# Wide passes of neighbouring products back to back in a split-fp32 SwiGLU kernel: products four and five, and seven and the next first

## The chip, the cores and the metric

The kernel runs on one core of a Trainium2 chip. The metric is device time in microseconds (us) of one execution. Before the change it is 1697.6 us, the median of three runs (1697.36 to 1698.68).

## What is computed

One layer of a trunk: RMS norm, forgetting attention with four heads, residual, RMS norm, SwiGLU, residual, final RMS norm; 512 tokens, width 2048, inner width 5632, all float32. The change touches the first half of SwiGLU only:

```python
def _swiglu(h, w_gate_up, w_down):
    gu = h @ w_gate_up                      # (512, 2048) @ (2048, 11264)
    g, u = gu[..., :D_FF], gu[..., D_FF:]
    return (jax.nn.silu(g) * u) @ w_down
```

## The kernel before

**Split operands.** Every float32 operand is taken as a high part, rounded to the fast float32 format of TensorE (fp32r), and a low part, the remainder. A product is high weights by high tokens, high weights by low tokens, and low weights by high tokens. In gate and up a product has 256 tokens. Its *wide pass* (L3075) runs the high weights against 512 columns, the 256 tokens' high and low parts side by side, eight matmuls for eight blocks of 128 rows. Its *narrow pass* (L3081) runs the low weights against the 256 columns of the high parts, eight matmuls into the left half of the same PSUM bank.

**Units of seven products.** A unit computes 128 columns of gate and the same 128 of up, for all 512 tokens, with seven products in place of eight (a Strassen-Winograd scheme). The token side (`SEVEN`: A11, S1, S2, A12, S3, S4, A22) is made once; the trace names it hT, oT, oT, hT, s, nothing, hT. The weight side of each product (`PART_OF`) is a loaded block of 1024 x 128 or a sum of such blocks: B11 alone, B11+B12, that plus B22 (both sums by DVE, L2410), B21 alone, B12+B22 (by an accumulating DMA that POOL issues, L1151), B22 alone, and a last one again by POOL. There are 41 units in this form: one opens, 36 run in a loop of four units per turn (`Fori`), four are unrolled at the end. Three more are computed plainly before them (L3059 and L3064), with 512 columns in every matmul. The down product with 512 columns throughout (L3126) follows.

**Who does what, per product.**
- ACT rounds the weight block into the high ring buffer (`part_hi`, L1617). The ring has two places, so it waits until the wide pass of the product two before has read its place (`highs_read`) and until DVE has made that product's low part.
- DVE subtracts it from the block, which gives the low part (`part_lo`, L2399). It waits for the high part (`t_hi`) and until the product two before is complete (`product`, which the last narrow matmul raises), since the low ring also has two places.
- PE waits for `t_hi` before a wide pass and for `t_lo` before a narrow one, and at some products for a bank: `combined` (DVE's combinations of banks, L2428) or `q_copied` (ACT's copies, L1641 and L1649).
- Each engine's order is written out by hand in its own `unit`, and an engine runs it strictly in that order. DVE's is: low part 2 (`unit_lo(at, 1)`), second sum, gate's right half of the unit before, low part 3, the product of gate and up of the unit before with its small sums (L2475, L2452), low part 4, the combination for product three's bank, low parts 5 and 6, and so on; at the end low part 1 and the first sum of the next unit.
- SP issues the loads of later units when a low part is made (`load_after`): that of B22 for the next unit after low part 6, of B21 after low part 7.

Products are counted from one in this text and from zero in the code: product four is `e == 3`, and low part four is `unit_lo(at, 3)`.

The functions that the change touches, and what calls them:

Of the kernel before, what the change touches and what calls it, by code (L numbers as in the profile page):

```python
# [216 lines left out]
def fox_layer(nc, x, norm_mix, w_in, b_f, w_out, norm_ffn, w_gu, w_down, norm_out, out):  # L217
# [10 lines left out]
    G = 4  # L228
# [32 lines left out]
    with ExitStack() as ctx:  # L261
# [3 lines left out]
        def sem(name):  # L265
            return ctx.enter_context(nc.semaphore(name))
# [121 lines left out]
        SEVEN = ((A11, 0), (S1, 1), (S2, 0), (A12, 3), (S3, 0), (S4, 2), (A22, 0))  # L388
# [6 lines left out]
        def bank_of(at, which):  # L395

            return UNIT_BANKS[0 if at.r is None else (at.u + 1) % 2][which]
# [5 lines left out]
        def whole(bank):  # L403

            return ps[:, bank, :].rearrange("p (n t) -> p n t", n=2)
# [178 lines left out]
        def is_last(r):  # L584

            return isinstance(r, int) and r == GROUPS - 2
# [117 lines left out]
        combined = sem("combined")  # L704
# [1174 lines left out]
        def _(dve):  # L1879
# [521 lines left out]
            def named_lo(r, n, name, i):  # L2401
                part_lo(r, n, slot(place(r, name, i)[0]))

            def unit_lo(at, e):
                named_lo(at.r, at.first + e, PART_OF[e], at.u)
# [12 lines left out]
            def second_sum(at):  # L2418

                dve.wait_ge(t_lo, at.part(1))  # L2420
                wait_loaded(dve, at.r, "B22", at.u)
                sum_of(at, "B11", "B22")

            def bank(at, which):
                return ps[:, bank_of(at, which), :]

            def combine(out, in0, in1, op):
                nc.vector.tensor_tensor(out, in0, in1, op).then_inc(combined, 1)  # L2428
# [5 lines left out]
            def gate_right_before(at):  # L2434

                dve.wait_ge(x_taken, at.taken(0))
                add_right(ga[:, HALF:S], bank_before(at))

            def plain_out(f, into):

                dve.wait_ge(silu_done, f + 1)
                if f:
                    dve.wait_ge(product, 4 * f)
                else:
                    wait_used(dve, At(FIRST_FFN + 1))
                nc.vector.tensor_tensor(into, ps[:, GU[f % 2][1], :], into, ALU.mult).then_inc(a_done, 1)
# [38 lines left out]
            def unit(at):  # L2485

                end = is_last(at.r) and at.u == G - 1
                unit_lo(at, 1)
                second_sum(at)
                if at.r is not None:  # L2490
                    gate_right_before(at)
                    unit_lo(at, 2)
                    act_before(at)
                else:
                    plain_out(2, third)
                    dve.wait_ge(a_copied, 2)
                    first_of_pair(0, 0)
                    second_of_pair(0, 0)
                    unit_lo(at, 2)
                unit_lo(at, 3)  # L2500
                if at.r is None:
                    dve.wait_ge(a_copied, 3)
                    first_of_pair(1, 4)
                dve.wait_ge(product, at.product(2))
                dve.wait_ge(q_copied, at.copied(2))
                combine(bank(at, 2), qq[:], bank(at, 0), ALU.subtract)
                unit_lo(at, 4)
                unit_lo(at, 5)
                if end:
                    wait_loaded(dve, at.r, "B21", at.u)  # L2510
                    dve.wait_ge(t_lo, at.part(2))
                    sum_of(at, "B11", "B21")
                dve.wait_ge(x_taken, at.taken(1))
                add_right(ga[:, 0:HALF], bank_of(at, 3))
                dve.wait_ge(product, at.product(4))
                combine(qq[:], qq[:], bank(at, 0), ALU.subtract)
                unit_lo(at, 6)
                dve.wait_ge(a_done, at.acts())
                dve.wait_ge(combined, at.combined(3))
                combine(cc[:, HALF:S], qq[:, 0:HALF], qq[:, HALF:S], ALU.add)  # L2520
                if not end:
                    unit_lo(at.next(), 0)
                    first_sum(at.next())
                if end:
                    operand_low(Down(None, 0), 0)
                    operand_low(Down(None, 0), 1)
                    down_lo(Down(None, 0), 0)
                    gate_right_before(at.next())
                    down_sum(Down(None, 0), 0)
                dve.wait_ge(x_taken, at.taken(2))  # L2530
                add_right(cc[:, 0:HALF], bank_of(at, 2))
# [154 lines left out]
            for u in range(G):  # L2686
                unit(Unit(GROUPS - 2, u))

            first = Down(None, 0)
# [29 lines left out]
        def _(pe):  # L2719
# [187 lines left out]
            first = At(0)  # L2907
# [157 lines left out]
                                           start=False, stop=second == 1 and k == QK8 - 1)  # L3065
                ins.then_inc(product, 1)

            def half_product(at, e):

                tokens, which = SEVEN[e]  # L3070
                n = at.first + e
                both = whole(bank_of(at, which))
                pe.wait_ge(t_hi, at.part(e))
                for k in range(QK8):
                    ins = nc.tensor.matmul(both, ring(at.r, 0, n)[:, k * P:(k + 1) * P],  # L3075
                                           tokens[2][:, :, k * HALF:(k + 1) * HALF],
                                           start=e < 2 and k == 0, stop=False, skip_group_check=True)
                ins.then_inc(highs_read, 1)
                pe.wait_ge(t_lo, at.part(e))
                for k in range(QK8):  # L3080
                    ins = nc.tensor.matmul(both[:, 0, :], ring(at.r, 1, n)[:, k * P:(k + 1) * P],  # L3081
                                           tokens[0][:, k * HALF:(k + 1) * HALF],
                                           start=False, stop=k == QK8 - 1, skip_group_check=True)
                ins.then_inc(product, 1)

            def unit(at):

                first = at.r is None
                if first:
                    pe.wait_ge(silu_done, 2)  # L3090
                else:
                    pe.wait_ge(combined, at.combined(-5))
                half_product(at, 0)
                if first:
                    pe.wait_ge(a_done, 2)
                    pe.wait_ge(s_lo, 12)
                half_product(at, 1)
                pe.wait_ge(q_copied, at.copied(1))
                half_product(at, 2)
                half_product(at, 3)  # L3100
                pe.wait_ge(combined, at.combined(1))
                half_product(at, 4)
                if first:
                    pe.wait_ge(s_lo, 16)
                half_product(at, 5)
                pe.wait_ge(combined, at.combined(3))
                half_product(at, 6)

            def down_product(dn, e):

# [35 lines left out]
            at = At(FIRST_FFN)  # L3146
# [55 lines left out]
```

## Time and profile before

| | |
|---|---|
| median of three runs | 1697.6 us |
| the profiled execution, its own time | 1697.54 us |
| its span, first to last instruction | 1695.7 us |
| PE busy (matmuls) | 1682.6 us, 99% |
| PEld busy (weight loads) | 1449.5 us, 85% |
| DVE busy | 1337.2 us, 79% |
| ACT busy | 853.8 us, 50% |
| POOL busy | 210.6 us, 12% |
| granted TensorE clock, mean | 0.998 |
| gate and up in units of seven | 465.38 to 1267.04 us |

Busy times are shares of the span. Matmuls are pipelined: a matmul row shows how long one is under way, which is longer than the distance from one to the next, so the stream's pace is read from starts, or from the chain of waits, and not from the mean of one. A row that groups eight matmuls has the time from the first start to the last end. Brackets give idle time of that engine before the row and what ended it.

### The profile page before, as it was taken

How to read it: one execution, taken by the hardware profiler on the slowest of the kernel's cores; microseconds unless marked ns; L12 is line 12 of the kernel's file. 1: busy time of each engine (PE TensorE's matmuls, PEld its weight loads, DVE VectorE, ACT ScalarE, POOL GpSimd, SP SyncE). 2: the span in 40 equal slices, each digit the busy share in tenths (PEclk: the TensorE clock that was granted, in tenths of full speed). 3: DMA queues.
4: the chain of work that ended last, by engine and by line, in shares of the span. 5: the costliest groups of instructions: out<-in, count | busy, mean ns of one | idle time of the engine just before them, and what ended most of it. 6: DMA issues, size and time to landing. Idle time of an engine off the chain costs nothing.

```text
span 1695.7 us, 25155 instructions
## 1 busy us (share of the span) xinstructions
PE 1682.6 (99%) x8977; PEld 1449.5 (85%) x8977; DVE 1337.2 (79%) x1485; ACT 853.8 (50%) x1075; POOL 210.6 (12%) x327
## 2 busy tenths in 40 slices
PE   9999999999999999999999999999999999999998
PEld 7888888888888888888888888888888888888886
DVE  6888778968877777777777777777789978878886
ACT  6454555444445454445454445454455444444454
POOL 1010102001011111111111111111100001000043
PEclk9999999999999999999999999999999999999999
DMA  8746667942277777776777776777788886867854
GB/s 236 168 100 162 149 150 218 316 100 74 73 208 180 186 186 186 195 187 174 186 181 204 195 195 177 186 187 185 197 241 244 251 240 194 253 178 192 257 156 146
DMA packets 311630, 317.55 MB, mean 187 GB/s; under 512 B 10256, under 2 KB 259360, under 8 KB 305168
## 3 DMA queue, kind: packets, MB, share of 16 engines
q1 hardware_dynamic: 291968, 231.79, 44.2%
q0 software_dynamic: 19152, 83.37, 25.0%
q10 hardware_dynamic: 448, 1.55, 0.3%
q8 instruction: 40, 0.66, 0.2%
q14 instruction: 22, 0.18, 0.0%
HBM read 205.83 MB, written 30.41 MB: 139 GB/s over the span
## 4 chain that ended last, share of the span: by engine, by line
PE 74%; DVE 1%; issue 0%; ACT 0%; POOL 0%; POOLq 0%; ACTq 0%; DVEq 0%
PE ps L3075 31%; PE ps L3126 23%; PE ps L3081 16%; PE ps L3059 2%; PE ps L3064 1%; PE ps L3041 1%; DVE split L2540 0%; DVE down_slot L2553 0%; PE ps L3045 0%; ACT split L1726 0%; DVE tmp L1907 0%; PE ps L2737 0%; DVE xres L2569 0%; ACT xres L1607 0%; POOL var L1233 0%
## 5 line engine op out<-in xcount | busy, mean ns | idle before, releaser
L1617 ACT ACTIVATE split<-raw 128x1024 fp32r<-128x1024 f32 x295 | 312.1, 1058 | 342.5 <-DVE raw L2410 112.9
L2399 DVE TENSOR_TENSOR split<-raw,split 128x1024 fp32r<-128x1024 f32 x295 | 360.5, 1223 | 139.1 <-ACT split L1617 135.0
L3126 PE MATMUL ps<-split,operand_hi 128*128 128x512 f32 x1232 | 380.5, 389 | 0.2
L3126 PEld LDWEIGHTS ps<-split,operand_hi 128*128 128x128 f32 x1232 | 231.2, 188 | 49.8 <-ACT split L1726 0.9
L3075 PE MATMUL ps<-hT,split 128*128 128x512 f32 x984 | 246.4, 392 | 0.0
L3126 PE MATMUL ps<-split,operand_lo 128*128 128x512 f32 x616 | 239.7, 389 | 0.0
L1726 ACT ACTIVATE split<-down_slot 128x2048 fp32r<-128x2048 f32 (+1 forms) x82 | 145.6, 1781 | 173.9 <-PE ps L3126 84.8
L3075 PEld LDWEIGHTS ps<-hT,split 128*128 128x128 f32 x984 | 177.0, 189 | 31.7
L2540 DVE TENSOR_TENSOR split<-down_slot,split 128x2048 fp32r<-128x2048 f32 (+1 forms) x84 | 177.2, 2109 | 19.8 <-ACT split L1726 16.2
L3075 PE MATMUL ps<-oT,split 128*128 128x512 f32 x656 | 164.3, 392 | 0.0
L3081 PEld LDWEIGHTS ps<-hT,split 128*128 128x128 f32 x984 | 134.2, 190 | 9.6
L3081 PE MATMUL ps<-hT,split 128*128 128x256 f32 x984 | 137.2, 282 | 0.0
L3126 PEld LDWEIGHTS ps<-split,operand_lo 128*128 128x128 f32 x616 | 115.7, 188 | 24.0
L3075 PEld LDWEIGHTS ps<-oT,split 128*128 128x128 f32 x656 | 118.0, 189 | 21.1
L1150 POOL TENSOR_TENSOR turn_of<-half 128x1 f32<-128x1 f32 x81 | 31.7, 391 | 738.4 <-DVE raw L2410 302.6
L2569 DVE TENSOR_TENSOR xres<-xres,ps 128x1024 f32<-128x1024 f32 (+1 forms) x72 | 86.7, 1204 | 40.3 <-PE ps L3126 39.8
L2410 DVE TENSOR_TENSOR raw<-raw 128x1024 f32<-128x1024 f32 x83 | 101.7, 1226 | 7.8
L1381 ACT ACTIVATE split<-raw 128x1024 fp32r<-128x1024 f32 x63 | 66.7, 1060 | 61.4 <-DVE raw L2040 26.2
L3081 PEld LDWEIGHTS ps<-oT,split 128*128 128x128 f32 x656 | 89.5, 190 | 6.4
L3081 PE MATMUL ps<-oT,split 128*128 128x256 f32 x656 | 91.5, 282 | 0.0
L2034 DVE TENSOR_TENSOR split<-raw,split 128x1024 fp32r<-128x1024 f32 x63 | 76.8, 1221 | 17.9 <-ACT split L1381 17.9
L3075 PE MATMUL ps<-s,split 128*128 128x512 f32 x328 | 82.1, 392 | 0.0
(281 smaller groups left out, 2469.3 us busy)
## 6 DMA issues: line engine op xcount, KB each, us to landing
raw<-in_ffn_w_gate_up_dram SPq DMA_DIRECT2D x172, 512.0 KB, 5.0
raw<-raw POOLq DMA_DIRECT2D x99, 512.0 KB, 4.5
down_slot<-in_ffn_w_down_dram SPq DMA_DIRECT2D x32, 1024.0 KB, 7.1
a_sums<-pack SPq DMA_DIRECT2D x22, 1024.0 KB, 6.4
raw<-in_fox_w_in_dram SPq DMA_DIRECT2D x36, 512.0 KB, 4.7
down_slot<-down_slot POOLq DMA_DIRECT2D x16, 1024.0 KB, 8.1
operand_raw<-a_sums SPq DMA_DIRECT2D x28, 512.0 KB, 7.3
down_slot<-in_ffn_w_down_dram SPq DMA_DIRECT2D x16, 768.0 KB, 6.5
```

Of the source, the lines that this page charges most:

```text
L1381: nc.scalar.activation(head_ring(0, n), head_part(at, e), ACT.Copy).then_inc(u_hi, 1)
L1617: nc.scalar.activation(ring(r, 0, n), source, ACT.Copy).then_inc(t_hi, 1)
L1726: nc.scalar.activation(down_ring(dn, 0, e), down_part(dn, DOWN_OF[e]), ACT.Copy).then_inc(d_hi, 1)
L2034: nc.vector.tensor_tensor(head_ring(1, n), head_part(at, e), f32(head_ring(0, n)), ALU.subtract).then_inc(u_lo, 1)
L2399: nc.vector.tensor_tensor(ring(r, 1, n), source, f32(ring(r, 0, n)), ALU.subtract).then_inc(t_lo, 1)
L2410: nc.vector.tensor_tensor(x1, x1, x2, ALU.add).then_inc(t_sum, 1)
L2540: nc.vector.tensor_tensor(down_ring(dn, 1, e), down_part(dn, DOWN_OF[e]), f32(down_ring(dn, 0, e)), ALU.subtract).then_inc(d_lo, 1)
L2569: nc.vector.tensor_tensor(part, part, down_banks(dn, which)[:, tiles, :], ALU.add if sign > 0 else ALU.subtract).then_inc(y_added, 1)
L3059: ins = nc.tensor.matmul(out, ring(None, 0, n)[:, k * P:(k + 1) * P], h_ffn[part][:, :, QK8 * second + k, :], start=second == 0 and k == 0 ...
L3075: ins = nc.tensor.matmul(both, ring(at.r, 0, n)[:, k * P:(k + 1) * P], tokens[2][:, :, k * HALF:(k + 1) * HALF], start=e < 2 and k == 0, s ...
L3081: ins = nc.tensor.matmul(both[:, 0, :], ring(at.r, 1, n)[:, k * P:(k + 1) * P], tokens[0][:, k * HALF:(k + 1) * HALF], start=False, stop=k ...
L3126: ins = nc.tensor.matmul(banks[:, tile, :], operand[e][part][:, i, tile * P:(tile + 1) * P], down_ring(dn, part_of_t, e)[:, i * BANK:(i + ...
```

## The change

PE runs the wide passes of products four and five one behind the other, and then their two narrow passes. It does the same with the seventh product of a unit and the first of the next. The last unit is left as it was in both places, and the opening unit begins with its own first product. On DVE the combination into product three's bank moves ahead of low part four. No instruction is added or taken away, the waits move with their passes, and neither ACT, POOL nor SP has another order.

```diff
 # DVE, unit(at)
-                unit_lo(at, 3)
                 if at.r is None:
                     dve.wait_ge(a_copied, 3)
                     first_of_pair(1, 4)
                 dve.wait_ge(product, at.product(2))
                 dve.wait_ge(q_copied, at.copied(2))
                 combine(bank(at, 2), qq[:], bank(at, 0), ALU.subtract)
+                unit_lo(at, 3)
                 unit_lo(at, 4)
 # PE: half_product is split into wide_passes (its first loop) and narrow_pass (its second)
+            def half_product(at, e):
+
+                wide_passes(at, e)
+                narrow_pass(at, e)
+
             def unit(at):
 
                 first = at.r is None
+                end = is_last(at.r) and at.u == G - 1
+                then = Unit(0, 0) if first else at.next()
                 if first:
                     pe.wait_ge(silu_done, 2)
-                else:
-                    pe.wait_ge(combined, at.combined(-5))
-                half_product(at, 0)
-                if first:
+                    half_product(at, 0)
                     pe.wait_ge(a_done, 2)
                     pe.wait_ge(s_lo, 12)
                 half_product(at, 1)
                 pe.wait_ge(q_copied, at.copied(1))
                 half_product(at, 2)
-                half_product(at, 3)
+                wide_passes(at, 3)
+                if end:
+                    narrow_pass(at, 3)
                 pe.wait_ge(combined, at.combined(1))
-                half_product(at, 4)
+                wide_passes(at, 4)
+                if not end:
+                    narrow_pass(at, 3)
+                narrow_pass(at, 4)
                 if first:
                     pe.wait_ge(s_lo, 16)
                 half_product(at, 5)
                 pe.wait_ge(combined, at.combined(3))
-                half_product(at, 6)
+                wide_passes(at, 6)
+                if not end:
+                    pe.wait_ge(combined, then.combined(-5))
+                    wide_passes(then, 0)
+                narrow_pass(at, 6)
+                if not end:
+                    narrow_pass(then, 0)
```

PE's order at products four and five of a unit in the loop, before (the tokens are hT for product four and s for product five):

```order
L3075 MATMUL ps<-hT,split 128x512 [waits t_hi]
L3075 MATMUL ps<-hT,split 128x512 x7
L3081 MATMUL ps<-hT,split 128x256 [waits t_lo]
L3081 MATMUL ps<-hT,split 128x256 x7
L3101 REGISTER_ALU
L3073 REGISTER_ALU [waits combined]
L3075 MATMUL ps<-s,split 128x512 [waits t_hi]
L3075 MATMUL ps<-s,split 128x512 x7
L3081 MATMUL ps<-s,split 128x256 [waits t_lo]
L3081 MATMUL ps<-s,split 128x256 x7
```

And the same place in the changed kernel (L3087 is the narrow pass now):

```order
L3075 MATMUL ps<-hT,split 128x512 [waits t_hi]
L3075 MATMUL ps<-hT,split 128x512 x7
L3113 ISA
L3073 REGISTER_ALU [waits combined]
L3075 MATMUL ps<-s,split 128x512 [waits t_hi]
L3075 MATMUL ps<-s,split 128x512 x7
L3087 MATMUL ps<-hT,split 128x256 [waits t_lo]
L3087 MATMUL ps<-hT,split 128x256 x7
L3087 MATMUL ps<-s,split 128x256 [waits t_lo]
L3087 MATMUL ps<-s,split 128x256 x7
```

The wide pass of product five, with its wait for DVE's combination, now stands ahead of the narrow pass of product four.

PE's order from a unit's seventh product to the next unit's first in the loop, before (both have tokens from hT):

```order
L3075 MATMUL ps<-hT,split 128x512 [waits t_hi]
L3075 MATMUL ps<-hT,split 128x512 x7
L3081 MATMUL ps<-hT,split 128x256 [waits t_lo]
L3081 MATMUL ps<-hT,split 128x256 x7
L3073 REGISTER_ALU [waits combined]
L3075 MATMUL ps<-hT,split 128x512 [waits t_hi]
L3075 MATMUL ps<-hT,split 128x512 x7
L3081 MATMUL ps<-hT,split 128x256 [waits t_lo]
```

And in the changed kernel:

```order
L3075 MATMUL ps<-hT,split 128x512 [waits t_hi]
L3075 MATMUL ps<-hT,split 128x512 x7
L3073 REGISTER_ALU [waits combined]
L3075 MATMUL ps<-hT,split 128x512 [waits t_hi]
L3075 MATMUL ps<-hT,split 128x512 x7
L3087 MATMUL ps<-hT,split 128x256 [waits t_lo]
L3087 MATMUL ps<-hT,split 128x256 x7
L3087 MATMUL ps<-hT,split 128x256 [waits t_lo]
L3087 MATMUL ps<-hT,split 128x256 x7
```

The seventh product's narrow pass, the last of whose matmuls says that the product is complete, stands behind the next unit's first wide pass.

DVE's order behind a unit's third low part, in a unit of the loop with three small sums (L2452), before:

```order
L2452 TENSOR_TENSOR pack<-pack 128x256 [waits pack_step]
L2394 REGISTER_ALU
L2399 TENSOR_TENSOR split<-raw,split 128x1024 [waits product,t_hi]
L2505 REGISTER_ALU [waits product]
L2428 TENSOR_TENSOR ps<-qq,ps 128x512 [waits q_copied]
L2394 REGISTER_ALU
L2399 TENSOR_TENSOR split<-raw,split 128x1024 [waits product,t_hi]
```

And in the changed kernel:

```order
L2452 TENSOR_TENSOR pack<-pack 128x256 [waits pack_step]
L2504 REGISTER_ALU [waits product]
L2428 TENSOR_TENSOR ps<-qq,ps 128x512 [waits q_copied]
L2394 REGISTER_ALU
L2399 TENSOR_TENSOR split<-raw,split 128x1024 [waits product,t_hi]
```

The combination (L2428), which waits for product three, has changed places with low part four.

## Rows read from the trace of the kernel before

**Rows 1.** Busy time, stage of gate and up: PE, PEld, DVE, ACT, POOL; clock; DMA
```profile
465.38:1267.04 801.66, 801.66 (x4593) 705.47 (x4592) 611.61 (x741) 403.24 (x535) 97.84 (x160) 1.00 0.74 191
```
**Rows 2.** Groups of instructions of that stage: count, busy us, mean ns, idle
```profile
L3075 PE MATMUL ps<-hT,split 128*128 128x512 f32 x984 | 246.4, 392 | 0.0
```
**Rows 3.** Chain of waits in that stage: start us, us, what
```profile
901.28 1.84 PE ps L3075 x8
903.12 0.95 PE ps L3081 x8
```
**Rows 4.** Chain of waits ahead of it: L3041 narrow, others wide
```profile
416.24 3.84 PE ps L3041 x32
...
427.47 3.63 PE ps L3059 x16
431.09 1.81 PE ps L3064 x8
```
**Rows 5.** Timeline of PE at a unit boundary: start us, us, what
```profile
912.29 2.00 PE L3075 MATMUL ps<-hT,split 128*128 128x512 f32 x8
914.13 1.11 PE L3081 MATMUL ps<-hT,split 128*128 128x256 f32 x8
...
920.67 2.00 PE L3075 MATMUL ps<-oT,split 128*128 128x512 f32 x8
```
**Rows 6.** Timeline of DVE there
```profile
916.37 1.23 DVE L2399 TENSOR_TENSOR split<-raw,split 128x1024 fp32r<-128x1024 f32 x1 [0.93 <-ACT split L1617]
917.72 1.23 DVE L2410 TENSOR_TENSOR raw<-raw 128x1024 f32<-128x1024 f32 x1
...
920.07 1.23 DVE L2399 TENSOR_TENSOR split<-raw,split 128x1024 fp32r<-128x1024 f32 x1 [0.79 <-ACT split L1617]
...
923.19 1.22 DVE L2399 TENSOR_TENSOR split<-raw,split 128x1024 fp32r<-128x1024 f32 x1
924.33 0.69 DVE L2428 TENSOR_TENSOR ps<-qq,ps 128x512 f32<-128x512 f32 x1
```
**Rows 7.** Timeline of ACT there
```profile
915.28 1.06 ACT L1617 ACTIVATE split<-raw 128x1024 fp32r<-128x1024 f32 x1 [2.41 <-DVE raw L2410]
...
918.98 1.06 ACT L1617 ACTIVATE split<-raw 128x1024 fp32r<-128x1024 f32 x1 [0.24 <-DVE raw L2410]
```
**Rows 8.** Timeline, a narrow pass and the DVE instruction that waits for it
```profile
908.54 1.11 PE L3081 MATMUL ps<-s,split 128*128 128x256 f32 x8
...
909.70 0.69 DVE L2428 TENSOR_TENSOR qq<-qq,ps 128x512 f32<-128x512 f32 x1 [1.10 <-PE ps L3081]
```
**Rows 9.** Chain of waits, down product, where PE waited for ACT
```profile
1302.85 1.50 ACT split L1726
...
1304.39 3.74 PE ps L3126 x15
```
**Rows 10.** Timeline of PE there: the ninth wide matmul behind the wait
```profile
1306.36 0.39 PE L3126 MATMUL ps<-split,operand_hi 128*128 128x512 f32 x1
```
**Rows 11.** Timeline, unrolled units: second low part, and third high part
```profile
1209.59 1.23 DVE L2399 TENSOR_TENSOR split<-raw,split 128x1024 fp32r<-128x1024 f32 x1 [0.80 <-ACT split L1617]
...
1212.11 1.06 ACT L1617 ACTIVATE split<-raw 128x1024 fp32r<-128x1024 f32 x1 [0.15 <-DVE raw L2410]
```
**Rows 12.** Timeline: low part six, load of B22, POOL's turn for it
```profile
926.60 1.23 DVE L2399 TENSOR_TENSOR split<-raw,split 128x1024 fp32r<-128x1024 f32 x1 [0.45 <-ACT split L1617]
...
927.99 0.37 SPq L905 DMA_DIRECT2D raw<-in_ffn_w_gate_up_dram  x1
...
935.09 0.18 POOL L1150 TENSOR_TENSOR turn_of<-half 128x1 f32<-128x1 f32 x1 [12.34 <-DMA raw<-in_ffn_w_gate_up_dram]
```
**Rows 13.** POOL's accumulating DMAs of that stage (L1151)
```profile
DMA to landing us min/median/max: 4.5/4.5/6.3
```
**Rows 14.** Waits of that stage: us in total, times, longest
```profile
POOL turn_of L1150 <- DMA raw<-in_ffn_w_gate_up_dram: 249.3, 20, 13.3
```
**Rows 15.** Busy time around the wait of rows 9, columns as in rows 1
```profile
1300.00:1310.00 10.00, 9.96 (x44) 7.87 (x43) 8.34 (x7) 6.31 (x5) 1.04 (x2) 1.00 1.03 284
```

More of the change, by code:

```diff
@@ L3066, in plain_part, with wide_passes @@
                 ins.then_inc(product, 1)
-            def half_product(at, e):
+            def wide_passes(at, e):
                 tokens, which = SEVEN[e]
@@ L3078, in half_product, with narrow_pass @@
                 ins.then_inc(highs_read, 1)
+            def narrow_pass(at, e):
+                tokens, which = SEVEN[e]
+                n = at.first + e
+                both = whole(bank_of(at, which))
                 pe.wait_ge(t_lo, at.part(e))
```

## The prediction

> **What bounds the kernel now.** I read the averages of the whole stage first, then the chain of waits, then the order of events across one unit boundary on PE, DVE and ACT. In the stage of gate and up, from 465.38 to 1267.04 us, PE is busy for all of its 801.66 us at clock 1.00, and DVE for 611.61 [rows 1]. The reader should see that nothing else counts there: the chain is PE alone, eight wide matmuls in 1.84 us, then eight narrow in 0.95, and so on [rows 3]. Three of a unit's seven products take their tokens from hT, with eight wide matmuls each, and there are 984 of these [rows 2]: 984 / 24 = 41 units. So the change can gain only by making PE's own stream shorter, and can lose wherever it makes PE wait, which it does not do now.
>
> **What the new order saves on PE.** A wide run behind narrow matmuls takes 1.84 us [rows 3]. Behind other wide ones it is cheaper: 16 wide in 3.63 and 8 in 1.81 in the stretch before the stage [rows 4]. Narrow ones go the other way, slightly: 32 in 3.84 are 0.12 each, so 0.96 for eight [rows 4], against the 0.95 behind wide ones [rows 3]. Each junction of two products that run as one thus saves 0.03 - 0.01 = 0.02 us. There are 80 junctions: products four and five, and seventh with next first, in 40 units each (the last unit has neither). 80 x 0.02 = 1.6 us. That is all the change can bring directly.
>
> The Trainium skill has a rule that would take even this away ("TensorE: Matmul & The Clock Gate", Back-to-back issue gap): an isolated warm matmul is followed by the next after its columns over 2.4 GHz and some 2.5 ns, whatever stands beside it. By it an estimate is 216 ns wide and 109 narrow with nothing for a junction, the saving is nought, and the sum below would come out 1.6 us higher. The trace does not agree: 227 ns and 120 ns in pure runs, and 1.84 against 1.81 us for the same eight [rows 3, 4]. I go by the rows.
>
> **What the new order delays.** The number of instructions stays. What moves is the end of a product: product four's narrow pass now runs behind product five's wide one, product seven's behind the next first's wide one, so each is complete 1.81 us later. Who waits for these two ends?
>
> At the unit boundary it is DVE's low part for the next unit's second product (it writes the ring buffer that the seventh product's narrow pass reads). Behind it hangs a chain: that low part, DVE's second sum (L2410, which waits for the low part), ACT's high part of the sum for the third product (L1617), and PE's wide pass of the third product. Take the boundary at 912.29 [rows 5]:
> - Before: the narrow pass of product seven starts at 914.13 and is out at 915.24, but DVE starts the low part only at 916.37, as ACT's high part runs from 915.28 to 916.34. Second sum at 917.72, ACT at 918.98 until 920.04, PE's wide pass at 920.67 [rows 5 to 7]. There is 0.63 us to spare, and the product's end isn't what releases DVE.
> - After: wide seven 912.29, wide next first 912.29 + 1.84 = 914.13, narrow seven 914.13 + 1.81 = 915.94, out 1.11 later, 917.05. DVE follows PE by 0.05 us: a narrow pass from 908.54 is out at 909.65, and DVE goes at 909.70 [rows 8]. So the low part starts at 917.10. From its start to the end of ACT's high part it is 920.04 - 916.37 = 3.67 us [rows 6, 7], every link of it a direct wait on the one before. The high part is then complete at 917.10 + 3.67 = 920.77.
> - PE without a wait would come to that wide pass at 915.94 + 0.95 + 0.96 + 1.84 + 0.95 = 920.64.
>
> What a late release costs PE is seen once in the stage of the down product: ACT's high part ends at 1302.85 + 1.50 = 1304.35, the matmul starts at 1304.39, and the eight wide behind it need until the ninth at 1306.36, so 1.97 us instead of the 1.84 behind a narrow run [rows 9, 10]. So PE starts at 920.77 + 0.04 = 920.81, 0.17 late, and loses 1.97 - 1.84 = 0.13 more while it gets going: 0.30 us at each boundary. It does not build up: from there everything hangs on PE again until the next seventh product.
>
> The chain is 3.67 for the 36 units inside the loop and shorter for the four of the last, unrolled group: 1212.11 + 1.06 - 1209.59 = 3.58 [rows 11], so 0.21 there. 36 x 0.30 + 4 x 0.21 = 11.6 us.
>
> **The other waits, by the same working.** Wide five moves forward by the 0.95 us of narrow four and now needs its high part and DVE's combination (L2428 into the bank of product three) by about 925.3. The combination now stands ahead of low part four, so it doesn't pay for that: from low part three to its own start it was 924.33 - 920.07 = 4.26, less the 1.14 from 923.19 of low part four, 3.12 [rows 6]. With low part three at 920.80 it could go at 923.92, needs product three's end anyway (about 923.9), and is done at about 924.7: 0.6 us or more before PE. Low part four starts then and ends at 925.9, needed at 927.4. Both are hidden. Here DVE idles in front of the combination and low parts four and five queue behind it; PE's narrow passes come 1.5 us and about 1 us after these, so nobody waits. The next first product's wide pass moves forward by 0.95; its high part waits for product six's wide pass and takes 1.06 [rows 7], and PE still has a narrow pass of 0.95 and wide seven of 1.84 to do in that time. The wait on the bank of the next first product is met a unit earlier. All these I cost at nothing; if one bound it would be by some 0.1 to 0.5 us per unit.
>
> Low part six waits for product four's end, now after wide five: narrow four starts at 920.67 + 2.79 + 1.84 + 1.81 = 927.11, out 928.22, so DVE goes at 928.27 (counted without the stall, which moves all of this alike) where it went at 926.60, 1.67 later [rows 12]. Behind it on SP stands the load of B22 for the next unit, issued at 927.99 and landed when POOL moves at 935.09 [rows 12]. It lands at about 936.8 now. DVE's second sum needs it at 938.0, and POOL's accumulating DMA is issued 0.4 later and takes 4.5, at most 6.3 [rows 13]: 941.7 to 943.5, against the start of the high part for product five, which must be by about 943.9. Hidden, but by the least of all.
>
> **The sum.** 1697.54 us is the profiled execution's own time (span 1695.7 and 1.8 around it), within 0.1 of the median of 1697.6, so the same sum serves for both: 1697.54 - 1.6 + 11.6 = 1707.5 us, 0.6% slower. What isn't shown: a stalled wide pass inside this stage. From below, PE loses only its lateness of 0.17 and no restart: 40 x 0.17 - 1.6 = +5.2, 1702.7. From above, DVE and ACT each lag 0.07 more than in these rows, as register waits stand between them in the loop, and the loss is 0.45: 40 x 0.45 - 1.6 = +16.4, 1713.9. I take 0.30, as each link has a row of its own.
>
> **Rivals.**
> - *No wait at all.* The saving stays and nothing is lost: 1697.54 - 1.6 = 1695.9, no change that could be measured. It decides by one figure: whether the chain from the seventh product's end to PE's need is under about 3.4 us (920.64 less the 0.2 us or so that a release must lead by, minus 917.05); I work it out at 3.72. For it: there are 0.63 us to spare before, and DVE's old wait for ACT swallows 1.1 of the 1.81 us; 0.33 us of error in the modelled ends of matmuls would be enough. Against it: DVE's start follows a modelled end by 0.05 in rows 8, so that end is no guess. Chance 0.12.
> - *A second wait, at product five.* If the later load of B22 makes POOL's addition late, ACT's high part and with it wide five come late, in the 20 units where POOL waits for such a load [rows 14]. The longest landing leaves 0.4 us, the median 2.2. If it missed by 0.5 in those 20, 10 us are added: 1717.5. For it: the load took 7.1 us in that unit and shares the DMA engines with the store of a pack. Against it: the addition takes 4.5 in the median. Chance 0.06.
> - *The clock.* PE idles for a moment in each of 40 units. If one product of each unit then ran at 1.2 instead of 2.4 GHz, it would take at most twice its 2.79 us: 40 x 2.79 = 112 more, about 1819. Against it: the stretch with the stall at 1304 has clock 1.00 throughout, with PE busy 9.96 of 10 us [rows 15]. The Trainium skill speaks for it (same page, A second HAM failure mode: psum-queue depth-cycling): short idle times of PE between groups of matmuls can make its clock swing between the two levels. No row here shows that happening. Chance 0.01.
>
> **How the numbers follow.** The forecast has 0.81, the rivals 0.12, 0.06 and 0.01. A measurement of this kernel can tell about 0.2%, 3.4 us, from no change. Faster by that (under 1694.2) needs more than the whole saving, so 0.02 for something unseen; the same (to 1701.0) is the first rival and the forecast's lowest edge, 0.14; slower is the rest, 0.84. The range is 1702.5 to 1714: the bounds above, which leave out the first rival, the upper two and a little of the forecast.
>
> **What would show it.** In the changed profile: wide runs of 16 in about 3.65 and narrow of 16 in about 1.91 in the chain; PE idle in front of L3075 with ACT's L1617 as what ended it, 40 times, each around 0.2 to 0.3 us in front of the third product and nowhere else; DVE's first low part of a unit released by PE instead of ACT; in the chain of waits, DVE's L2399 and L2410 and ACT's L1617 appear once per unit. A unit takes 19.55 - 0.04 + 0.30 = 19.8 us. The forecast is wrong if that wide pass starts without idle time, if idle time stands in front of product five, or if PEclk falls below 9.

## The result

The changed kernel takes 1710.78 us (median of 6, 1709.35 to 1711.07), the kernel before on the same chips 1697.53 (6 runs, 1697.36 to 1698.68). The ratio is 1.0073 with an interval of 1.0063 to 1.0084: 13.2 us slower, inside the range of 1702.5 to 1714 and 3.3 us above the forecast of 1707.5.

The two profiled executions are 1710.96 and 1697.54 us. Of the 13.4 between them the stage of gate and up has 12.1. Busy time of the changed kernel in that stage, columns as in [rows 1]:

```profile
466.73:1280.52 813.79, 811.24 (x4594) 707.66 (x4592) 608.89 (x741) 404.84 (x535) 98.68 (x160) 1.00 0.72 188
```

The stage is 813.79 us long where it was 801.66 [rows 1]. PE, which had no idle moment there, now has some, and the clock is 1.00 as before. The down product behind it takes as long in both. The other 1.35 us is ahead of the stage (and 0.1 the other way behind it); it begins at 466.73 and not at 465.38. It lies in the first transposes, which are the same code in both kernels. PE there, the kernel before, and then the changed one:

```profile
5.82 1.72 PE L2751 MATMUL ps<-ident,xres 128*128 128x128 f32 x14 [1.05 <-DMA xres<-in_x_dram]
```
```profile
5.84 3.22 PE L2751 MATMUL ps<-ident,xres 128*128 128x128 f32 x14 [0.76 <-DMA xres<-in_x_dram]
```

Fourteen transposes took 1.72 us in one execution and 3.22 in the other: their starts are 109 ns apart in the first and 213 in the second, where they become 109 too a little later. What differs is when TensorE's clock rises. The trace of the kernel before has its first clock entry, at full speed, at 4.32 us, that of the changed kernel at 9.80; a stretch ahead of the first entry is printed as 1.00 by the profile, so its row doesn't tell. In all eleven kept profiles these transposes start 109 ns apart behind that entry and 213, twice as far, ahead of it, and the entry comes at 4.3 to 5.8 us or at 9.3 to 10.1. So ahead of it the engine runs at half its pace, the lower of the clock's two levels, as far as the starts can tell. The code there is the same in every version, so this is no part of the change. Runs of the kernel before mostly fall in two groups some 1.3 us apart (of 27 runs, 11 at 1697.3 to 1697.6 and 13 at 1698.6 to 1699.9), so below I compare the length of the stage, from its first matmul to the first of the down product. It is free of that.

The chain of waits of the changed kernel over one unit boundary, start us, us, what:

```profile
920.26 3.65 PE ps L3075 x16
923.91 0.97 PE ps L3087 x8
924.88 0.03 issue
924.91 0.02 DVEq L2398
924.93 0.04 issue
924.98 1.23 DVE split L2399
926.21 0.03 issue
926.24 0.04 DVEq L528
926.28 0.04 issue
926.32 1.24 DVE raw L2410
927.56 0.02 issue
927.58 1.07 ACT split L1617
928.65 0.04 issue
928.69 2.14 PE ps L3075 x8
```

Where the chain was PE alone [rows 3], it leaves PE at the end of product seven's narrow pass and goes through low part two, the second sum and high part three, link by link as forecast, back to PE's wide pass of product three. Of the forecast's four figures, three can be read off it: the wide run of 16 is 3.65, the way from low part two's start to the end of the high part is 928.65 - 924.98 = 3.67, and ACT's end leads PE's start by 0.04. The fourth is off: between product seven's end and low part two stand 0.10 us and not 0.05 (0.11 from the modelled end of the last matmul), with an instruction of DVE's sequencer (DVEq L2398) in between. What PE's weight loads wait for in the stage (us in total, times, longest):

```profile
PEld ps L3075 <- ACT split L1617: 9.5, 36, 0.3
PEld ps L3075 <- issue: 1.0, 4, 0.3
PEld ps L3087 <- DVE split L2399: 0.5, 1, 0.5
```

36 waits in the loop and 4 in the unrolled units, all in front of product three. There is a 41st, which I did not forecast, on a narrow pass.

A unit from product one's wide pass to the next is 19.867 us at 27 boundaries of the loop, 19.800 at nine (every fourth), and 19.83 in the unrolled units; it was 19.553. At the nine low part two starts 0.04 us behind product seven's end, at the 27 and at the four unrolled ones 0.11 behind it.

### The profile page after: what moved, and what is told of

Its sections match the earlier page's. It is cut to its first block, busy times and chain, and to the rows that moved or that the text cites. A ratio compares the mean times of both kernels' runs of the same rounds, so it can differ in the third digit from the quotient of the medians.

```text
span 1709.1 us, 25146 instructions
## 1 busy us (share of the span) xinstructions
PE 1693.8 (99%) x8977; PEld 1453.4 (85%) x8977; DVE 1334.3 (78%) x1485; ACT 855.3 (50%) x1075; POOL 211.2 (12%) x327
## 4 chain that ended last, share of the span: by engine, by line
PE 68%; DVE 5%; ACT 2%; issue 1%; POOL 0%; DVEq 0%; POOLq 0%; ACTq 0%
PE ps L3075 28%; PE ps L3147 23%; PE ps L3087 13%; DVE split L2399 2%; DVE raw L2410 2%; PE ps L3059 2%; ACT split L1617 2%; PE ps L3064 1%; PE ps L3041 1%; PE ps L3045 0%; DVE split L2540 0%; DVE tmp L1907 0%; PE ps L2737 0%; ACT xres L1607 0%; DVE down_slot L2553 0%
## 5 line engine op out<-in xcount | busy, mean ns | idle before, releaser
L3075 PE MATMUL ps<-hT,split 128*128 128x512 f32 x984 | 238.8, 391 | 0.0
L3075 PE MATMUL ps<-oT,split 128*128 128x512 f32 x656 | 169.2, 400 | 2.5
L3087 PEld LDWEIGHTS ps<-hT,split 128*128 128x128 f32 x984 | 128.9, 191 | 6.9 <-DVE split L2399 0.5
L3087 PE MATMUL ps<-hT,split 128*128 128x256 f32 x984 | 131.1, 283 | 0.1
L3087 PEld LDWEIGHTS ps<-oT,split 128*128 128x128 f32 x656 | 89.2, 190 | 6.8
L3087 PE MATMUL ps<-oT,split 128*128 128x256 f32 x656 | 90.9, 281 | 0.0
L3075 PE MATMUL ps<-split 128*128 128x512 f32 x328 | 82.1, 392 | 0.0
```

## The experiments

**Each part alone.** Only the boundary: `unit` on PE keeps `half_product(at, 3)` and `half_product(at, 4)`, and DVE its old order.

```diff
-                wide_passes(at, 3)
-                if end:
-                    narrow_pass(at, 3)
+                half_product(at, 3)
                 pe.wait_ge(combined, at.combined(1))
-                wide_passes(at, 4)
-                if not end:
-                    narrow_pass(at, 3)
-                narrow_pass(at, 4)
+                half_product(at, 4)
```

> Only the seventh product and the next first run as one; products four and five and DVE's order are as before. The stage is the time from the first L3075 matmul to the first matmul of the down product: 801.66 us before, 813.78 changed. Theory (the late end of product seven delays DVE's low part two, its second sum, ACT's high part three and so PE): all of the loss is here, and only half of the saving: 40 x 0.02 = 0.8 off, and 27 x 0.37 + 9 x 0.28 + 4 x 0.33 = 13.8 on, so a stage of 814.6 and some 1710.6 in all, with PE idle before product three in 40 units and nowhere else. Rival (the combination ahead of low part four, or the early wide five, makes the wait): no idle time, a stage of 800.9 and 1696.8.

Measured: 1710.48 us (4 runs, ratio 1.0073, 1.0058 to 1.0089), the whole of the loss. Its stage, and then the waits of its weight loads:

```profile
465.56:1279.42 813.86, 811.29 (x4594) 707.93 (x4592) 608.70 (x741) 407.71 (x535) 97.21 (x160) 1.00 0.73 188
```
```profile
PEld ps L3075 <- ACT split L1617: 9.6, 36, 0.3
PEld ps L3075 <- issue: 1.0, 4, 0.3
```

The 40 waits are all here, and the 41st isn't. The rival, that the other part makes them, is out. The stage is 0.7 us shorter than expected: the eight wide matmuls behind the wait take 1.94 to 1.95 us in the loop here, and 1.98 at 27 boundaries of the changed kernel. Why they differ is open.

Only products four and five: the boundary is as before.

```diff
-                wide_passes(at, 6)
-                if not end:
-                    pe.wait_ge(combined, then.combined(-5))
-                    wide_passes(then, 0)
-                narrow_pass(at, 6)
-                if not end:
-                    narrow_pass(then, 0)
+                half_product(at, 6)
```

> Only products four and five run as one, with DVE's new order; the unit boundary is as before. Theory: 40 x 0.02 = 0.8 saved; in the last unit, where PE keeps its order but DVE has the new one, low part four is late once and costs 0.45, so a stage of 801.3 and some 1697.2 in all. Rival (this part makes the wait): a stage near 813 and 1709.

Measured: 1697.10 us (11 runs) against 1698.31 (27), ratio 0.9996 (0.9987 to 1.0005), which can't be told from no change. The stage tells more:

```profile
466.87:1268.05 801.18, 801.11 (x4593) 706.12 (x4592) 609.80 (x741) 400.26 (x535) 100.09 (x160) 1.00 0.73 191
```

801.18 against 801.66: 0.48 shorter. One wait is left, and it is in the last unit. The timeline of this kernel there:

```profile
1256.55 2.00 PE L3075 MATMUL ps<-hT,split 128*128 128x512 f32 x8
1256.75 0.70 DVE L2428 TENSOR_TENSOR ps<-qq,ps 128x512 f32<-128x512 f32 x1 [1.47 <-PE ps L3087]
1257.36 2.35 DVE L2399 TENSOR_TENSOR split<-raw,split 128x1024 fp32r<-128x1024 f32 x2
1258.63 1.21 PE L3087 MATMUL ps<-hT,split 128*128 128x256 f32 x8
```

PE keeps its old order in the last unit and wants low part four right behind wide four, at 1258.4. DVE has the new order, sits idle for product three's end until 1256.75, and starts low part four at 1257.36. It ends 1.2 us later, and PE's narrow pass starts at 1258.63, too late by 0.2. The expected price was 0.45 us; the next run gives it as 0.33.

The same with DVE's old order in the last unit:

```diff
+                if end:
+                    unit_lo(at, 3)
                 ...
                 combine(bank(at, 2), qq[:], bank(at, 0), ALU.subtract)
-                unit_lo(at, 3)
+                if not end:
+                    unit_lo(at, 3)
```

> As the one with only products four and five, but DVE makes low part four ahead of the combination in the last unit, as before. Theory: the one wait in the last unit goes, nothing is left but the saving: a stage of 800.9, 0.45 less than without this, and some 1696.8. If that wait had another cause than DVE's order, the stage stays at 801.3.

Measured: 1696.94 us (11 runs) against 1698.31, ratio 0.9993 (0.9984 to 1.0002).

```profile
466.63:1267.48 800.85, 800.85 (x4593) 706.17 (x4592) 609.77 (x741) 400.16 (x535) 101.31 (x160) 1.00 0.73 191
```

PE is without idle time again, and the 0.33 us of the last unit are back. 801.66 - 800.85 = 0.81 for 40 junctions is 0.020 each, as the rows of runs behind narrow and behind wide ones gave.

**Taking away what low part two waits for.** Low part seven is written over its own raw block (B11), so it leaves the ring, product seven's narrow pass reads it there, and low part two can go as soon as product six is complete. The last unit has the old order on DVE.

```diff
+        low_seven = {n: placed(f"low_seven{n}", 96 + 4 * n, [P, PART], F32R) for n in (0, 2)}
 # DVE, unit_lo
-                    dve.wait_ge(product, parts(r, n - 1))
+                dve.wait_ge(product, parts(at.r, n - 2 if e == 1 and at.r is not None else n - 1))
 # SP, load_after
                 if more > 1:
+                    sp.wait_ge(product, at.product(6))
                     load_part(at.r, "B11", at.u + 2)
```

> Both pairs run as one, but low part seven is written over its own block in the B11 slot and not into the ring, so low part two of the next unit no longer waits for product seven (SP's load into that slot waits for it instead, two units ahead of its use). Low part four in the last unit is as before. Theory: low part two starts when ACT's high part is there, as before the change, PE idles in none of the 40 units, and 80 junctions save 0.02 each: a stage of 800.1 and some 1696.0. Rival (PE waits at product three for another reason, as ACT's copy or the gate's half that follow product seven): the stage stays near 813. Rival (the later load of B11 collides with others): PE idles in front of product seven or one.

Measured: 1697.63 us (11 runs, 1696.31 to 1700.49) against 1698.31, ratio 0.9996 (0.9987 to 1.0005). The 40 waits are gone, so the theory holds, but something else came, and not where the expectation's rival had it (products seven or one); the runs spread further, too. Its stage, then what its weight loads wait for, then the timelines of PE, ACT, POOL and SP around the longer of the two waits:

```profile
466.79:1270.04 803.25, 800.68 (x4594) 705.44 (x4592) 609.92 (x741) 404.58 (x535) 99.17 (x160) 1.00 0.76 191
```
```profile
PEld ps L3091 <- ACT split L1625: 3.4, 2, 2.0
```
```profile
1065.44 2.11 PE L3091 MATMUL ps<-s,split 128*128 128x512 f32 x8 [1.56 <-ACT split L1625]
...
1064.33 2.01 ACT L1625 ACTIVATE split<-raw 128x1024 fp32r<-128x1024 f32 x2 [3.80 <-DMA raw<-raw]
...
1055.71 0.86 POOL L1159 DMA_DIRECT2D raw<-raw  x1 [1.00 <-issue]
...
1055.66 0.37 SPq L911 DMA_DIRECT2D raw<-in_ffn_w_gate_up_dram  x1
```

PE waits twice in front of product five (tokens s), at 556 and 1065 us, for ACT's high part, which waited for POOL's accumulating DMA. Issued at 1055.71, it landed 8.5 us later, where the median is 5.0; in front of the other wait it took 7.5. SP's load of B11 was issued at 1055.66, and 0.5 us ahead of that other addition. So what the second rival of the prediction would have led to, a late addition for product five, is seen here, but not by its cause: it is a load beside the addition, and not a late load of B22.

So the load moves behind low part three of the next unit (for that unit's successor, into the same slot):

```diff
 # SP, load_after
+                if more:
+                    sp.wait_ge(t_lo, at.part(2))
+                    load_part(at.r, "B11", at.u + 1)
                 ...
-                if more > 1:
-                    sp.wait_ge(product, at.product(6))
-                    load_part(at.r, "B11", at.u + 2)
```

> Low part seven in place as before, but SP issues the load of B11 behind low part three of the next unit instead of at the end of product seven. In the run before, PE waited twice in front of product five (1.3 and 1.8 us): POOL's accumulating DMA, issued at 1055.7, landed only at about 1064.3, and the load of B11 had been issued beside it at 1055.5. Theory (the load of B11 slows POOL's addition for product five): with the load some 4 us later both waits are gone, the stage is 800.1, the median 1696.0 to 1696.6, and the spread is that of the kernel before. Rival (that addition is late now and then for another reason): one to three such waits stay, a stage of 801 to 804.

Measured: 1696.69 us (11 runs, 1695.77 to 1697.87) against 1698.52 (15), ratio 0.9991 (0.9982 to 1.0001).

```profile
465.30:1265.39 800.09, 800.09 (x4594) 705.84 (x4593) 609.60 (x741) 404.73 (x535) 103.86 (x160) 1.00 0.73 191
```

No idle time is left, and 801.66 - 800.09 = 1.57 for 80 junctions is again 0.020 each. This is the whole of the gain that both pairs can bring. Its stage is the shortest here, though whole runs hardly tell it from the kernel before: 1.6 us is 0.09%, and the start alone moves a run by 1.3 us. The collision as such is not gone, only moved to where nobody is late for it. POOL's additions in the stage:

```profile
DMA to landing us min/median/max: 4.5/5.0/8.5
```

By their issues in this trace they are of two kinds: 39 have a load of B11 issued 0.4 to 0.6 us ahead of them, and 38 of these take 5.8 to 6.5 us and one 8.5; the other 41 take at most 5.1, and 4.5 in the median. In the kernel before, where no addition has a load within 0.6 us of it, the longest is 6.3 [rows 13]. So a load beside an addition slows it, which is what the theory of this run says; why single ones take 7.5 or 8.5 is open.

**The 0.12 us at DVE.** The 0.12 and 0.05 of the expectation are the 0.11 and 0.04 above, with the end of product seven read 0.01 us earlier. The changed kernel with the two waits of a low part in the other order:

```diff
-                dve.wait_ge(t_hi, parts(r, n + 1))
                 ...
                     dve.wait_ge(product, parts(r, n - 1))
+                    dve.wait_ge(t_hi, parts(r, n + 1))
```

> The changed kernel with the two waits of every low part in the other order on DVE: first for the product two before, then for the high part. In the changed kernel 27 of the 40 late low parts start 0.12 us behind the end of product seven, with a sequencer instruction of DVE (L2398) between the two, and the nine of the loop's first unit 0.05 behind it, with none. Theory (DVE's sequencer stands at the first wait and has one more instruction to run when it is released; the last wait goes with the subtraction): where the late wait stands matters. If the product is waited for by an instruction of its own now, all 36 start 0.12 behind and nine units get 0.07 longer, a stage of 814.4; if instead it is the one that goes with the subtraction, all start 0.05 behind and the stage is 27 x 0.07 = 1.9 shorter, 811.9. Rival (the 0.12 is the way from PE to DVE and has nothing to do with the waits): the stage stays at 813.8.

Measured: 1710.29 us (4 runs, ratio 1.0071, 1.0055 to 1.0086). The stage:

```profile
466.02:1280.48 814.46, 810.77 (x4594) 707.97 (x4592) 609.51 (x741) 404.81 (x535) 97.26 (x160) 1.00 0.72 188
```

814.46, 0.67 longer, as the first branch had it. The chain of waits of this kernel between product seven and low part two:

```profile
923.86 0.97 PE ps L3088 x8
924.82 0.03 issue
924.85 0.04 DVEq L2399
924.89 0.04 issue
924.93 1.24 DVE split L2400
```

Now a register instruction of the sequencer takes the wait, and it stands between at every boundary of the loop: the nine that had 0.04 have 0.13, and their units are 19.887 us. In the four unrolled units it went the other way: there the subtraction takes the wait now, it starts 0.04 behind product seven's end, and the unit is 19.75 to 19.76 where it was 19.83. So both branches of the expectation are seen, in different units. A wait that is late costs some 0.07 us more where a sequencer instruction of its own takes it than where the subtraction does. Swapping them by hand makes it worse in all.

The kernel before shows the same turned round. There the wait for ACT's high part is the late one. At the nine boundaries low part two starts 0.12 us behind it (954.39 + 1.06 = 955.45), at all others 0.03 [rows 6, 7]:

```profile
954.39 1.06 ACT L1617 ACTIVATE split<-raw 128x1024 fp32r<-128x1024 f32 x1 [2.41 <-DVE raw L2410]
955.57 1.23 DVE L2399 TENSOR_TENSOR split<-raw,split 128x1024 fp32r<-128x1024 f32 x1 [1.02 <-ACT split L1617]
```

So which of the two waits goes with the subtraction could be read at each boundary ahead of the change.

**The chain alone, in the kernel before.** Nothing of the change, but DVE gets more to do between low part two and the second sum: one addition of 128x256, or three of 128x128, or six of 128x64.

```diff
                 unit_lo(at, 1)
+                for out in (root_row[:, HALF:HALF + P], root_row[:, HALF + P:S], ident[:]):
+                    nc.vector.tensor_tensor(out, f32(A22[0][:, 0:P]), f32(A22[0][:, 0:P]), ALU.add)
                 second_sum(at)
```

> The kernel before, with one more addition of 128x256 on DVE between low part two and the second sum of every unit, its result used nowhere. The chain grows by some 0.15 to 0.35 us, since part of the addition lies in the 0.12 that the second sum waits anyway. Theory: the slack of 0.33 takes it up, the stage stays at 801.7 or gets longer by less than 2 us. Rival (every delay of this chain costs PE as much): 40 x 0.25, a stage of 811 or more.

> The kernel before, with three more additions of 128x128 on DVE between low part two and the second sum of every unit; nothing else changes, and their results are used nowhere (one goes over the identity, which is dead by then). They lengthen the same chain by an amount x that the trace will show, some 0.4 to 0.7 us. ACT's high part three ends 0.53 us ahead of PE's wide pass in 28 of the units and 0.63 in nine, and a release has to lead by 0.2. Theory: no loss up to x = 0.33 (0.43 in the nine), from there a loss of x - 0.33 - 0.03 for the start and 0.13 for getting going; at x = 0.6 that is 0.3 or so per unit, a stage of 811 to 813, with PE idle before product three. Rival (the loss in the changed kernel comes from the long wide runs and not from the chain): no idle time, a stage of 801.7.

> The kernel before, with six more additions of 128x64 on DVE between low part two and the second sum of every unit, results used nowhere. With one addition of 128x256 the chain grew by 0.13 us and the stage stayed at 801.66; with three of 128x128 it grew by 0.40 and the stage by 0.48. Here the chain should grow by x of 0.55 to 0.65. Theory: 27 units in the loop had 0.53 us between ACT's high part three and PE, so PE's matmul starts x + 0.05 - 0.53 late and needs 0.13 to get going: at x = 0.6 some 0.12 + 0.13 = 0.25 each; nine had 0.63 and lose about 0.1 less; the four unrolled ones had 0.80 and lose next to nothing. A stage of 807 to 810. That the first 0.4 cost almost nothing and the next 0.2 most of a quarter microsecond per unit is what makes it a chain with slack. Rival (a delay here costs in proportion, or PE has other work to fill in): a stage under 803.

Measured, one run each: 1697.35 us with one, 1699.76 with three, 1705.45 with six. DVE's timeline and then the stage, with one:

```profile
916.29 1.23 DVE L2399 TENSOR_TENSOR split<-raw,split 128x1024 fp32r<-128x1024 f32 x1 [0.93 <-ACT split L1617]
917.43 0.42 DVE L2490 TENSOR_TENSOR root_row<-hT 128x256 f32<-128x256 f32 x1
917.76 1.22 DVE L2410 TENSOR_TENSOR raw<-raw 128x1024 f32<-128x1024 f32 x1
```
```profile
465.29:1266.95 801.66, 801.66 (x4594) 705.52 (x4593) 620.68 (x782) 403.33 (x535) 97.15 (x160) 1.00 0.74 191
```

With three:

```profile
918.06 1.23 DVE L2399 TENSOR_TENSOR split<-raw,split 128x1024 fp32r<-128x1024 f32 x1 [0.93 <-ACT split L1617]
...
919.81 1.22 DVE L2410 TENSOR_TENSOR raw<-raw 128x1024 f32<-128x1024 f32 x1
```
```profile
466.77:1268.91 802.14, 802.14 (x4593) 705.72 (x4592) 630.27 (x864) 403.09 (x535) 96.94 (x160) 1.00 0.74 191
```

With six (and what its weight loads wait for, where the wait is over 0.15 us):

```profile
920.99 1.22 DVE L2399 TENSOR_TENSOR split<-raw,split 128x1024 fp32r<-128x1024 f32 x1 [0.93 <-ACT split L1617]
...
922.95 1.22 DVE L2410 TENSOR_TENSOR raw<-raw 128x1024 f32<-128x1024 f32 x1
```
```profile
465.57:1275.01 809.44, 809.44 (x4594) 707.56 (x4593) 638.00 (x987) 402.98 (x535) 97.61 (x160) 1.00 0.74 189
```
```profile
PEld ps L3078 <- ACT split L1617: 4.1, 26, 0.2
```

From low part two to the second sum it was 1.35 us [rows 6] and is now 1.47, 1.75 and 1.96, so the chain is 0.12, 0.40 and 0.61 longer; the stage is 0.00, 0.48 and 7.78 us longer. The first two fifths of a microsecond are all but free, the next two tenths cost 7.3 us: a chain with slack, in the kernel before too. The price of a late release is confirmed apart from the change. I had put the edge at 0.33; at 0.40 the loss was 0.5 us and not the 4 to 5 that my figures give, so the run with three missed its expectation of 811 to 813. This execution at one of the 27 boundaries that had 0.53 us to spare (they are not the 27 of the longer hand-off):

```profile
940.71 1.06 ACT L1617 ACTIVATE split<-raw 128x1024 fp32r<-128x1024 f32 x1 [0.73 <-DVE raw L2410]
941.91 2.03 PE L3077 MATMUL ps<-oT,split 128*128 128x512 f32 x8
```

ACT's end leads PE's start by 0.14 there, PE is not late, and its eight wide matmuls take 1.85 to 1.87 us and not 1.84. With a lead of 0.24 or more they take 1.84, and at 0.05, where PE waits, 1.94 to 1.98. So a release need not lead by 0.2: down to some 0.14 it costs a few hundredths, and the full price of getting going comes with the wait. "28 of the units" in the expectation should read 27.

## Why the prediction was right, and what was off

- *The saving.* 80 x 0.02 = 1.6 us. Right: 1.57 when nothing else happens. The Trainium skill's formula ("TensorE: Matmul & The Clock Gate", Back-to-back issue gap) depends on the columns alone, and by it the saving would be nought. The section gives it for an isolated gap and sets streams of weight loads and matmuls apart from it; this stream, at 227 and 120 ns [rows 4] and with 0.020 us saved at each junction, doesn't follow it.
- *The chain at the boundary.* Right in every link but the hand-offs below, and shown from three sides: the boundary alone has all of the loss, another place for low part seven takes all 40 waits away, and lengthening the same chain makes them without the change.
- *From product seven's end to low part two: 0.05.* This is the step that was mis-sized. It was read from a combination whose wait goes with the instruction itself [rows 8]. It holds at nine boundaries of the loop; at the other 27 and the four unrolled ones it is 0.07 more, and 27 x 0.07 = 1.9 us. The upper bound had named it ("register waits stand between them"). A low part has two waits, and in these traces one stands in an instruction of DVE's sequencer and the other goes with the subtraction.
- *Loss per boundary: 0.30 and 0.21.* Against 19.513 us, the unit of the version without waits, it is 0.354 in the 27, 0.287 in the nine with the short hand-off, and 0.32 in the four unrolled. 27 x 0.354 + 9 x 0.287 + 4 x 0.32 = 13.4 where I had 11.6. The restart was right: eight wides behind the wait take 1.98 us in the 27 and 1.95 in the nine (1.97 from [rows 9, 10]). In the unrolled units I had 0.21, and the 0.11 more can be taken apart: 0.07 is the hand-off to DVE as above, 0.09 a hand-off from ACT to PE of 0.14 us in place of 0.05, as PE's wait for the high part stands in a sequencer instruction of its own there, and 0.05 goes off, as the eight wides take 1.92. ACT's high part three and PE's wide pass in such a unit:

```profile
1225.25 1.06 ACT L1617 ACTIVATE split<-raw 128x1024 fp32r<-128x1024 f32 x1 [1.05 <-DVE raw L2410]
1226.46 2.08 PE L3075 MATMUL ps<-oT,split 128*128 128x512 f32 x8
```

- *The other waits at nothing.* Right in 40 units and wrong in one. In the last unit PE's order stays while DVE's changes, and I had worked the combination's move out only for units where narrow four moves too. It costs 0.33 us.
- *The sum.* 13.4 + 0.3 - 1.6 = 12.1, which is the stage's 12.13; forecast was 10.0. The rest of the 13.2 between the medians, 1.1 us, is of the size of the steps at the start, which vary from run to run and are no part of the change: of the 3.3 us by which the forecast is off, 2.1 belong to it and the rest is chance.
- *The rivals.* No wait: out. Its condition asked for a lead of 0.2 us, where 0.14 cost next to nothing, and its 0.63 us to spare are those of the boundary worked out; at 27 others of the loop it is 0.53. The sum uses neither. The clock: 1.00 in the stage with 40 short idle times; the Trainium skill's warning of a clock that swings with short idle times ("TensorE: Matmul & The Clock Gate", A second HAM failure mode: psum-queue depth-cycling) was not borne out by waits of 0.2 to 0.3 us every 20. The second wait at product five: not in the changed kernel. A wait there came in the version with low part seven in place, where a load was issued 0.05 us beside POOL's addition: the same place, by another cause.

## What to carry to other kernels

Running two like passes back to back saves where their change-over costs, and delays the end of the first product. Before doing so, ask who waits for that end, follow the chain back to the engine that bounds, and compare its length with the work that engine has in the meantime: here 20 ns were saved at each junction and 290 to 350 lost at each boundary. If the delayed end frees a buffer, another place for one operand can be enough; and when an order is changed on one engine, look at every variant of the loop body (here the last unit) where its partner's order is not changed.

## What the runs showed of the hardware

- Wide matmuls (512 columns) behind narrow ones come in 1.84 us for eight, behind wide ones in 1.81; 256-column ones at 0.12 us each, eight in 0.95 behind wide ones and 0.96 behind narrow ones.
- An engine that takes a late wait by an instruction of its sequencer starts its work some 0.07 us later (DVE) or 0.09 (PE) than one whose wait goes with the work.
- Eight wide matmuls of gate and up take 1.92 to 1.98 us behind a wait and 1.84 without one; where the release comes 0.14 us ahead of PE they take 1.85 to 1.87.
- POOL's accumulating DMA lands 4.5 us after its issue in the median, and 5.8 to 6.5 (once 8.5) where a load was issued 0.4 to 0.6 us ahead of it.
- Fourteen transposes in the first 10 us take 1.72 or 3.22 us from one execution to the next, at 109 or 213 ns each. The slower ones lie ahead of the trace's first entry of the clock, which comes at 4.3 to 5.8 us or at 9.3 to 10.1; a stretch without an entry is printed as 1.00.
